# Group norm of a state-space stage: sums by a full block of ones, root and reciprocal on whole tiles

## The chip, the cores and the metric

One core of a Trainium2 chip runs the whole program. Its engines work side by side, each on its own instruction stream: TensorE (PE; PEld is its weight load), VectorE (DVE), ScalarE (ACT), GpSimd (POOL) and SyncE (SP, which issues the DMAs). They wait for each other by semaphores. The metric is the device time of one execution in microseconds (us).

## What is computed

The kernel is one step of a decoder layer for 512 new prompt tokens and 8 decode tokens (one for each of 8 sequences), so 520 tokens in all: an input norm and projection, sparse attention, a state-space branch (SSD) in 8 groups, a gated merge and a feed-forward part. The change lies in the norm at the end of the state-space branch. Each of its 8 groups has 256 channels, and each group is normalised by itself, token by token:

```python
y = y + d_skip.astype(F32).reshape(SSM_GROUPS, HEADS_PER_GROUP)[..., None] * xs
y = y.reshape(b, t, D_INNER) * jax.nn.silu(z.astype(F32))
yg = y.reshape(b, t, SSM_GROUPS, D_INNER // SSM_GROUPS)
yg = yg * lax.rsqrt(jnp.mean(yg * yg, axis=-1, keepdims=True) + EPS)
y = yg.reshape(b, t, D_INNER) * ssm_norm_w.astype(F32)
```

## The kernel before

Channels lie on the 128 partitions and the 520 tokens on the free axis, so a group's gated result `Y` is two tiles of 128x520, and a mean over channels is a sum over partitions, which TensorE makes by a matmul with ones.

The program is written by hand, one stream for each engine, and all streams have the same shape in this stage: a function `group(g, prev, more)`, called for group 0, then in a loop over groups 1 to 6, then for group 7. While group g's state work runs, TensorE also projects the six 128-channel tiles of group g + 1 (`D(0)` to `D(5)`, 8 steps of 128 rows each, two halves of 260 columns, f32, each half issued as two passes); in group 7 these are tiles for the merge gate. The order of the pieces is fixed by the order in the code.

A group runs like this. VectorE and ScalarE make the causal convolution (L1773, L1384) and the SiLU: a tanh on ScalarE (L1405) and a multiply on VectorE (L1780), four of each. GpSimd computes the convolution of the decode tokens (`dconv`, L2197 its last addition), for which the first tanh waits, and decays the decode states (L2202). TensorE turns B and the two x tiles by transposes (`step_turn`, L911 and L916), VectorE multiplies them by dt (`xdt`, L1791) and by the decay. TensorE spreads the decode tokens' B and C over the partitions (`step_decode`, L928); VectorE updates and reads the decode states (L1810 to L1824). TensorE multiplies C and B (`step_cb`, L936), VectorE masks the product (`CBm`, L1826). Then four chunks of 128 tokens: TensorE spreads the cumulative decay (`step_a`, L945), ScalarE makes exponentials of it (L1370 to L1374), GpSimd multiplies them with `CBm` (L2208), and TensorE forms the output and the state increment of the chunk (`step_y`, L958 to L964). VectorE carries the state `hT` from chunk to chunk: a copy for chunk 0 (L1835), a multiply and an add for the others (L1837, L1840); `step_y(c)` waits for the state of chunk c - 1. `Y` follows at the end (L1847 to L1855).

Between these pieces VectorE also runs four rounds of a top-8 search for the decode attention (`top`, L1734 to L1743), 12 pieces of 2.3 us, at fixed places: one piece behind the SiLU, two behind `xdt`, six behind `CBm`, three between the chunks.

The norm of group g - 1 runs inside group g. ScalarE squares the two `Y` tiles (L1379) and GpSimd adds them (L2175). TensorE sums over the partitions with the squares as weights and one column of ones as the moving operand (`sum_squares`, L410): the result is one number for each token, tokens on the partitions, five columns of PSUM. ScalarE takes the root of these 128x4 and 8x1 numbers (`root_norm`, L426), VectorE the reciprocal (`recip_norm`, L432). TensorE then spreads them back to all partitions (`spread_norm`, L418 and L419) and ScalarE copies the result out of PSUM into `rbg`, 128x520 (`copy_norm`, L436 and L437). VectorE multiplies `Y` by the gain and `rbg` (`norm`, L1756). On TensorE the sums stand behind `D(0)` and the spread behind `D(1)`, ahead of `step_turn`, since the x tiles are turned into the two PSUM banks that the norm uses.

Of the kernel before, what the change touches and what calls it, by code (L numbers as in the profile page):

```python
# [20 lines left out]
ACT = mybir.ActivationFunctionType  # L21
# [6 lines left out]
D = 1024  # L28
# [3 lines left out]
TH = T // 2  # L32
# [7 lines left out]
NG = 8  # L40
# [36 lines left out]
def build(nc, x_prompt, x_sample, cache_k, cache_v, cache_idx_k, state_ssm, state_conv, page_table,  # L77
# [5 lines left out]
    with ExitStack() as ctx:  # L83
# [22 lines left out]
        eps = sb("eps", [P, 1])  # L106
# [296 lines left out]
        NORM2, NORMF = NG + 1, NG + 2  # L403

# [29 lines left out]
        def copy_norm(act, e, out):  # L434
            act.wait_ge(S("norm_spread"), e + 1)
            act.activation(out[:, 0:SEQ], ps[:, 7, :], ACT.Copy).then_inc(S("norm_copied"), 1)  # L436
            act.activation(out[:, SEQ:T], ps[:, 6, 8:8 + NB], ACT.Copy).then_inc(S("norm_copied"), 1)  # L437
# [21 lines left out]
        def rms_dve(v, i, e, w_col):  # L459

            recip_norm(v, e)
            v.wait_ge(S("norm_copied"), 2 * e + 2)
# [208 lines left out]
        def _(pe):  # L671
# [229 lines left out]
            def step_norm(g):  # L901

                pe.wait_ge(S("sqg_added"), g + 1)
                sum_squares(pe, g + 1, sqg[:, 0, :])

            def step_turn(g, prev):
# [5 lines left out]
                if prev:  # L912
                    pe.wait_ge(S("norm_copied"), 2 * g + 2)
# [53 lines left out]
            def group(g, prev, more):  # L967
# [3 lines left out]
                D(0, 4, 8)  # L971
                if prev:
                    step_norm(g - 1)
                D(1)
                if prev:
                    spread_norm(pe, g)
# [32 lines left out]
            spread_norm(pe, NG)  # L1009
# [26 lines left out]
            pe.wait_ge(S("norm_copied"), 2 * NG + 2)  # L1036
# [194 lines left out]
        def _(act):  # L1231
# [148 lines left out]

            def group(g, prev, more):
# [16 lines left out]
                act.activation(dAs, ps[:, 4, 112:128].rearrange("p (i c) -> p i c", c=NB), ACT.Exp).then_inc(S("aux_read"), 1)  # L1398
                for i in range(4):
# [8 lines left out]
                if prev:  # L1408
                    root_norm(act, g, 256)
# [6 lines left out]
                if prev:  # L1416
                    copy_norm(act, g, rbg)
# [29 lines left out]
            root_norm(act, NG, 256)  # L1447
            copy_norm(act, NG, rbg)
# [124 lines left out]
        def _(v):  # L1573
# [178 lines left out]

            def norm(g):
                v.wait_ge(S("norm_copied"), 2 * g + 4)
# [5 lines left out]
            def group(g, prev, more):  # L1760
# [21 lines left out]
                if prev:  # L1782
                    recip_norm(v, g)
                    top(g, 0)
                    norm(g - 1)
                else:
                    top(g, 0)
# [29 lines left out]
                for j in range(2):  # L1817
                    v.wait_ge(S("state_new"), 2 * g + 2)
                    if j:
# [7 lines left out]
                                tri.unsqueeze(1).broadcast_to((P, 4, P)), ALU.mult).then_inc(S("CBm_ready"), 1)  # L1827
                top(g, 3, 4, 5, 6, 7, 8)
# [34 lines left out]
            recip_norm(v, NG)  # L1863
# [428 lines left out]
```

## Time and profile before

| what | us |
|---|---|
| time, median of 3 runs (1709.55 to 1717.97) | 1709.66 |
| the profiled execution | 1707.82 |
| its span, first to last instruction | 1706.0 |
| TensorE busy | 1612.1 (94%) |
| VectorE busy | 892.3 (52%) |
| ScalarE busy | 408.1 (24%) |
| GpSimd busy | 217.3 (13%) |

The span is cut at the first and the last instruction; the profiled execution's own time has 1.82 us around it. Busy time counts matmuls, weight loads and the like, not waiting. Matmul records overlap in the pipeline, so the distance of their starts, not their length, tells what one costs. TensorE's granted clock is the share of full speed that the chip gave it: 1.00 is 2.4 GHz, 0.50 is 1.2 GHz. A timeline row gives the start, the time to the end of the last of the merged instructions, the engine, the line, the operation, output<-input, form and count; in brackets stands the idle time of the engine before it and what ended it.

### The profile page before, as it was taken

Reading aid. Unit: us, or ns where it says so; the run is one execution under the profiler, and the core shown is the slowest. Engines: PE = TensorE matmul, PEld = TensorE weight load, DVE = VectorE, ACT = ScalarE, POOL = GpSimd, SP = SyncE. Lnnn points to the kernel's source line nnn. Section 1 sums busy time; section 2 is a strip of 40 time slices with the busy share of each in tenths; the row PEclk is TensorE's granted clock in tenths of the full one; section 3 lists DMA queues with packets and bytes.
Section 4 is the critical chain, followed back from the end, with each engine's and each line's share of the span. In section 5 each row is a group of like instructions: output and inputs, shape, how many; then the busy total and the mean of one; then the engine's idle time right before and its main releaser. Section 6 shows DMA issues by size and latency. Waiting matters only on the chain. (4 is left out here: it accounts for less than half of the span.)

```text
span 1706.0 us, 21649 instructions
## 1 busy us (share of the span) xinstructions
PE 1612.1 (94%) x8147; PEld 1366.3 (80%) x8147; DVE 892.3 (52%) x1412; ACT 408.1 (24%) x909; POOL 217.3 (13%) x224
## 2 busy tenths in 40 slices
PE   6998998899999899998998999999979999999997
PEld 5886786787877778777776888888868888888886
DVE  3313886349898898989987100010143444435232
ACT  3113316322243432434333011000112121210002
POOL 1000110022231322313222150000000000000000
PEclk7999999999999999999998999899989999999998
DMA  6111113123133131331212443212212232321211
GB/s 205 50 37 51 37 50 114 36 84 100 54 91 98 56 94 46 95 99 32 84 47 74 145 131 99 75 51 77 79 66 75 74 99 75 99 68 44 97 40 50
DMA packets 153489, 131.21 MB, mean 77 GB/s; under 512 B 11410, under 2 KB 149938, under 8 KB 153410
## 3 DMA queue, kind: packets, MB, share of 16 engines
q1 hardware_dynamic: 150610, 121.93, 23.6%
q0 software_dynamic: 2816, 8.39, 1.7%
q8 instruction: 46, 0.75, 0.2%
q14 instruction: 17, 0.14, 0.0%
HBM read 117.26 MB, written 13.27 MB: 77 GB/s over the span
## 5 line engine op out<-in xcount | busy, mean ns | idle before, releaser
L382 PE MATMUL ps<-xn,ring 128*128 128x260 f32 (+1 forms) x2752 | 635.7, 388 | 6.0 <-ACT work L1268 1.9
L382 PEld LDWEIGHTS ps<-xn,ring 128*128 128x128 f32 (+1 forms) x2752 | 521.3, 192 | 91.4 <-ACT work L1268 2.3
L1110 PE MATMUL ps<-xn,ring 128*128 128x260 f32 x528 | 124.8, 387 | 6.3 <-DVE xn L464 6.3
L1110 PEld LDWEIGHTS ps<-xn,ring 128*128 128x128 f32 x528 | 101.3, 192 | 22.1 <-issue 6.4
L382 PE MATMUL ps<-ssm_o,ring 128*128 128x260 f32 x512 | 114.6, 386 | 0.0
L382 PEld LDWEIGHTS ps<-ssm_o,ring 128*128 128x128 f32 x512 | 98.2, 192 | 15.2
L2208 POOL TENSOR_TENSOR ring<-ring 128x512 f32<-128x512 f32 x32 | 40.5, 1265 | 333.6 <-ACT ring L1374 333.6
L1110 PE MATMUL ps<-uT,ssm_o 128*128 128x260 f32 x352 | 81.1, 384 | 0.0
L1110 PEld LDWEIGHTS ps<-uT,ssm_o 128*128 128x128 f32 x352 | 67.3, 191 | 10.5
L1734 DVE MAX8 work<-work 8x8 f32<-8x2049 f32 x32 | 72.8, 2274 | 0.6
L1739 DVE FIND_INDEX8 dix<-work 8x8 uint32<-8x2049 f32 x32 | 72.8, 2274 | 0.0
L1741 DVE MATCH_REPLACE8 work<-work 8x2049 f32<-8x2049 f32 x32 | 72.5, 2266 | 0.0
L1523 ACT ACTIVATE uT<-ps 128x260 f32<-128x260 f32 x88 | 34.0, 387 | 154.3 <-PE ps L1110 154.3
L1773 DVE SCALAR_TENSOR_TENSOR work<-work 128x512 f32<-128x512 f32 x96 | 67.0, 768 | 7.3 <-ACT work L1384 7.3
L1872 DVE SCALAR_TENSOR_TENSOR work<-work 128x520 f32<-128x520 f32 x8 | 5.6, 700 | 118.7 <-ACT work L1464 118.7
L382 PE MATMUL ps<-uT,ring 128*128 128x260 f32 x256 | 58.8, 392 | 0.4 <-DVE uT L1922 0.4
L1161 PE MATMUL ps<-work,ring 128*128 128x260 f32 x264 | 59.2, 382 | 0.0
L2097 DVE TENSOR_TENSOR xT<-xT,ps 128x260 f32<-128x260 f32 x28 | 11.9, 424 | 86.2 <-PE ps L1161 86.2
L382 PEld LDWEIGHTS ps<-uT,ring 128*128 128x128 f32 x256 | 49.9, 196 | 8.5 <-DVE uT L1922 0.5
L1161 PEld LDWEIGHTS ps<-work,ring 128*128 128x128 f32 x264 | 50.2, 190 | 7.7
L382 PE MATMUL ps<-work,ring 128*128 128x260 f32 x256 | 56.3, 382 | 0.0
L1370 ACT ACTIVATE ring<-ps,work 128x128 f32<-128x128 f32 x128 | 36.5, 367 | 79.3 <-PE ps L945 79.3
(340 smaller groups left out, 2223.5 us busy)
## 6 DMA issues: line engine op xcount, KB each, us to landing
ring<-in_w_in SPq DMA_DIRECT2D x34, 1024.0 KB, 5.4
ring<-in_w_ffn_gate SPq DMA_DIRECT2D x11, 1024.0 KB, 5.3
ring<-in_w_ffn_up SPq DMA_DIRECT2D x11, 1024.0 KB, 5.3
ring<-in_w_in SPq DMA_DIRECT2D x16, 512.0 KB, 5.3
work<-in_state_ssm SPq DMA_DIRECT2D x16, 512.0 KB, 6.4
out<-work SPq DMA_DIRECT2D x16, 512.0 KB, 4.0
ring<-in_w_ssm_br SPq DMA_DIRECT2D x8, 1024.0 KB, 7.6
ring<-in_w_ffn_down SPq DMA_DIRECT2D x8, 1024.0 KB, 5.0
```

The lines of the kernel that those rows point to most:

```text
L382: mm = pe.matmul(ps[0:m, 2 * pair + h, 0:TH], lhs[k], rhs[k][:, h * TH:(h + 1) * TH], start=(k == 0), stop=(k == len(lhs) - 1))
L1110: mm = pe.matmul(ps[:, bank, 0:TH], lhs[:, k, :], rhs[:, k, :], start=start and k == 0, stop=k == 3, skip_group_check=not start)
L1161: mm = pe.matmul(ps[:, bank, 0:TH], lhs[k], rhs[k], start=start and k == 0, stop=k == KD - 1, skip_group_check=not start)
L1370: act.activation(M2[:, c % 2, r * P:(r + 1) * P], abc[:, r * P:(r + 1) * P], ACT.Relu, scale=-1.0, bias=atg[:, c, r:r + 1]).then_inc(S("E_ ...
L1523: act.activation(snap[:, i, :], ps[:, bank, 0:TH], ACT.Copy).then_inc(S("snapshot_taken"), 1)
L1734: v.max(best, row).then_inc(S("dtop_max"), 1)
L1739: v.max_index(dix[:], best, row).then_inc(S("dtop_index"), 1)
L1741: v.match_replace(row, best, row, -3.3e38).then_inc(S("dtop_cut"), 1)
L1773: v.scalar_tensor_tensor(xc[:, i, 0:SEQ], raw[:, i, t:t + SEQ], cw[:, 5 * i + t:5 * i + t + 1], xc[:, i, 0:SEQ], ALU.mult, ALU.add).then_i ...
L1872: v.scalar_tensor_tensor(m, gt, 1.0, m, ALU.add, ALU.mult).then_inc(S("mixed"), 1)
L2097: v.tensor_tensor(part, part, ps[:, bank, 0:TH], ALU.add).then_inc(S("down_added"), 1)
L2208: g.tensor_tensor(m, m, CBm[:, c:c + 1, :].broadcast_to((P, 4, P)), ALU.mult).then_inc(S("M_ready"), 1)
```

## The change

Per group, the sums are made by a full 128x128 block of ones as weights and the added squares as moving operand, 260 columns at a time, into PSUM banks 6 and 7 (`step_norm`). Every partition then holds the sum of every token, so no spread is needed. ScalarE takes the root from PSUM straight into `rbg` (`root_group`, two pieces of 128x260) and VectorE the reciprocal in place (`recip_group`, two pieces of 128x260), ahead of the same `norm`. `sum_squares`, `spread_norm` and the rest stay for the three other norms.

The pieces also move. On TensorE the sums now stand behind `step_aux`, ahead of the second half of `D(0)`, and the turn of the x tiles waits for the root alone. On ScalarE the root stands ahead of the four tanh, not behind them. On VectorE reciprocal and norm stand behind `CBm`, not ahead of `xdt`. Behind the last group the root, the reciprocal and the norm follow the sums as before, without the spread.

```diff
         NORM2, NORMF = NG + 1, NG + 2
+        SPREADS = {0: 1, NORM2: 2, NORMF: 3}
...
         def copy_norm(act, e, out):
-            act.wait_ge(S("norm_spread"), e + 1)
+            act.wait_ge(S("norm_spread"), SPREADS[e])
...
             def step_norm(g):
 
                 pe.wait_ge(S("sqg_added"), g + 1)
-                sum_squares(pe, g + 1, sqg[:, 0, :])
+                for h in range(2):
+                    mm = pe.matmul(ps[:, 6 + h, 0:TH], ones, sqg[:, 0, half[h]], start=True, stop=True)
+                mm.then_inc(S("norm_summed"), 1)
...
                 if prev:
-                    pe.wait_ge(S("norm_copied"), 2 * g + 2)
+                    pe.wait_ge(S("norm_root"), 2 * g + 2)
                 for c in range(4):
...
                 D(0, 0, 4)
                 step_aux(g, prev)
-                D(0, 4, 8)
                 if prev:
                     step_norm(g - 1)
+                D(0, 4, 8)
                 D(1)
-                if prev:
-                    spread_norm(pe, g)
                 step_turn(g, prev)
...
             step_norm(NG - 1)
-            spread_norm(pe, NG)
...
+            def root_group(g):
+
+                act.wait_ge(S("norm_summed"), g + 1)
+                for h in range(2):
+                    act.activation(rbg[:, half[h]], ps[:, 6 + h, 0:TH], ACT.Sqrt, scale=1.0 / 256,
+                                   bias=eps[:, 0:1]).then_inc(S("norm_root"), 1)
+
...
                 act.activation(dAs, ps[:, 4, 112:128].rearrange("p (i c) -> p i c", c=NB), ACT.Exp).then_inc(S("aux_read"), 1)
+                if prev:
+                    root_group(g)
                 for i in range(4):
...
                 act.activation(wexp, wexp, ACT.Exp).then_inc(S("wexp_ready"), 1)
-                if prev:
-                    root_norm(act, g, 256)
...
-                if prev:
-                    copy_norm(act, g, rbg)
                 act.wait_ge(S("turned"), g + 1)
...
+            def recip_group(g):
+
+                v.wait_ge(S("norm_root"), 2 * g + 2)
+                for h in range(2):
+                    v.reciprocal(rbg[:, half[h]], rbg[:, half[h]]).then_inc(S("norm_recip"), 1)
+
             def norm(g):
-                v.wait_ge(S("norm_copied"), 2 * g + 4)
+                v.wait_ge(S("norm_recip"), 2 * g + 4)
...
-                if prev:
-                    recip_norm(v, g)
-                    top(g, 0)
-                    norm(g - 1)
-                else:
-                    top(g, 0)
+                top(g, 0)
...
                                 tri.unsqueeze(1).broadcast_to((P, 4, P)), ALU.mult).then_inc(S("CBm_ready"), 1)
+                if prev:
+                    recip_group(g)
+                    norm(g - 1)
                 top(g, 3, 4, 5, 6, 7, 8)
...
-            recip_norm(v, NG)
+            recip_group(NG)
             norm(NG - 1)
```

TensorE in the loop over groups 1 to 6, from the last transposes of `step_aux` to the turn, before (L382 are the tiles; `ps` is PSUM, `work` and `cst` hold the squares, the ones and the identity):

```order
L898 MATMUL ps<-cst,work 128x128 x2
L382 MATMUL ps<-xn,ring 128x260 x8
L410 MATMUL ps<-cst,work 128x1 [waits sqg_added]
L410 MATMUL ps<-cst,work 128x1 x3
L410 MATMUL ps<-cst,work 8x1
L377 REGISTER_ALU
L382 MATMUL ps<-xn,ring 128x260 [waits dense_read]
L382 MATMUL ps<-xn,ring 128x260 x15
L416 ISA
L418 MATMUL ps<-cst,rt 128x128 [waits norm_recip]
L418 MATMUL ps<-cst,rt 128x128 x3
L419 MATMUL ps<-cst,rt 128x8
```

The same place after the change:

```order
L899 MATMUL ps<-cst,work 128x128 x2
L906 MATMUL ps<-work,cst 128x260 [waits sqg_added]
L906 MATMUL ps<-work,cst 128x260
L382 MATMUL ps<-xn,ring 128x260 x8
L377 REGISTER_ALU
L382 MATMUL ps<-xn,ring 128x260 [waits dense_read]
L382 MATMUL ps<-xn,ring 128x260 x15
L912 REGISTER_ALU [waits ctok_ready]
L914 MATMUL ps<-cst,work 128x128 [waits silu_done]
L914 MATMUL ps<-cst,work 128x128 x3
L916 ISA
L919 MATMUL ps<-cst,work 128x128 [waits norm_root]
```

The sums have moved up by 8 matmuls and are two instead of five; the five spread matmuls with their wait for the reciprocal are gone, and the turn waits for the root.

VectorE in the same loop, from the SiLU multiplies to the `xdt` products, before:

```order
L1780 SCALAR_TENSOR_TENSOR work<-work 128x520 [waits th_ready] x4
L432 RECIPROCAL rt<-rt 128x4 [waits norm_root]
L432 RECIPROCAL rt<-rt 8x1
L1734 MAX work<-work 8x8 [waits dtop_cut]
L1754 ISA
L1756 ISA [waits norm_copied]
L1756 REGISTER_ALU
L1756 SCALAR_TENSOR_TENSOR ssm_o<-work,cwg 128x520
L1756 ISA
L1756 REGISTER_ALU
L1756 SCALAR_TENSOR_TENSOR ssm_o<-work,cwg 128x520
```

After the change the same stretch reads, with `xdt` (L1796) right behind the search:

```order
L1790 SCALAR_TENSOR_TENSOR work<-work 128x520 [waits th_ready] x4
L1738 MAX work<-work 8x8 [waits dtop_cut]
L1794 REGISTER_ALU
L1796 TENSOR_TENSOR xdt<-ps,work 128x512 [waits turned]
L1796 TENSOR_TENSOR xdt<-ps,work 128x512
```

Reciprocal and norm, with their waits for the root and the copy, have left this place.

VectorE further on in the group, from `CBm` (L1826, L1831 after the change) to the search behind it, before:

```order
L1826 TENSOR_TENSOR ring<-ps,cst 128x512 [waits cb_done]
L1734 MAX work<-work 8x8 [waits dtop_cut]
L1739 MAX_INDEX dix<-work 8x8 [waits dtop_max,dtop_kept]
L1741 MATCH_REPLACE work<-work 8x2049
L1743 ISA [waits dtop_index]
```

and after:

```order
L1831 TENSOR_TENSOR ring<-ps,cst 128x512 [waits cb_done]
L1761 RECIPROCAL work<-work 128x260 [waits norm_root]
L1761 RECIPROCAL work<-work 128x260
L1764 ISA
L1766 ISA [waits norm_recip]
L1766 REGISTER_ALU
L1766 SCALAR_TENSOR_TENSOR ssm_o<-work,cwg 128x520
L1766 ISA
L1766 REGISTER_ALU
L1766 SCALAR_TENSOR_TENSOR ssm_o<-work,cwg 128x520
L1738 MAX work<-work 8x8 [waits dtop_cut]
```

The two reciprocals, now 128x260, and the norm stand between the mask and the searches.

## Rows read from the trace of the kernel before

**Rows 1.** Windows by group: stretch, length, busy by engine, PEclk, DMA share, GB/s.

```profile
430.61:857.73 427.12, 401.78 (x2318) 337.49 (x2317) 387.72 (x457) 150.42 (x343) 116.53 (x108) 0.98 0.28 78
430.61:500.75 70.14, 67.18 (x388) 56.08 (x387) 64.56 (x77) 25.09 (x58) 19.41 (x18) 0.98 0.29 80
```

**Rows 2.** Waits, 390 to 936 us: who waited for whom, total, times, longest.

```profile
PE ps L418 <- DVE rt L432: 20.0, 7, 3.1
```

**Rows 3.** Timeline of TensorE in one group, 575 to 642 us.

```profile
575.17 3.67 PE L382 MATMUL ps<-xn,ring 128*128 128x260 f32 x16
...
590.06 1.35 PE L418 MATMUL ps<-cst,rt 128*128 128x128 f32 x8 [3.10 <-DVE rt L432]
...
594.40 7.18 PE L382 MATMUL ps<-xn,ring 128*128 128x260 f32 x32
601.42 3.73 PE L928 MATMUL ps<-cst,work 128*128 128x128 f32 x32
...
629.04 0.45 PE L958 MATMUL ps<-ring,xdt 128*64 128x128 f32 x4
...
636.60 0.70 PE L964 MATMUL ps<-ring 128*128 128x256 f32 x2
```

**Rows 4.** Timeline of VectorE in the same group.

```profile
587.97 0.70 DVE L1780 SCALAR_TENSOR_TENSOR work<-work 128x520 f32<-128x520 f32 x1 [0.15 <-ACT work L1405]
...
589.93 2.27 DVE L1734 MAX8 work<-work 8x8 f32<-8x2049 f32 x1
592.92 1.43 DVE L1756 SCALAR_TENSOR_TENSOR ssm_o<-work,cwg 128x520 f32 x2 [0.71 <-ACT work L437]
594.60 1.29 DVE L1791 TENSOR_TENSOR xdt<-ps,work 128x512 f32<-128x512 f32 x2 [0.26 <-PE ps L916]
...
603.40 1.22 DVE L1810 TENSOR_TENSOR ring<-ps,work 128x1024 f32<-128x1024 f32 x1 [1.51 <-PE ps L928]
...
613.56 0.69 DVE L1826 TENSOR_TENSOR ring<-ps,cst 128x512 f32<-128x512 f32 x1
...
616.63 0.08 DVE L1739 MATCH_VALUE_LOAD dix<-work 8x8 f32 x1 [0.18 <-DVE work L1734]
...
628.45 0.40 DVE L1835 COPY work<-ps 128x256 f32<-128x256 f32 x1
...
637.47 0.41 DVE L1837 TENSOR_TENSOR work<-work 128x256 f32<-128x256 f32 x1
```

**Rows 5.** Line L1620, a reciprocal on a whole tile: ns min/median/max, first and last start.

```profile
L1620 DVE RECIPROCAL work<-work x1: 3403/3403/3403, 105.6 to 105.6; 128x520 f32<-128x520 f32 x1
```

**Rows 6.** Line L1780, and the timeline of GpSimd at two places.

```profile
L1780 DVE SCALAR_TENSOR_TENSOR work<-work x32: 685/699/2389, 375.4 to 873.6; 128x520 f32<-128x520 f32 x32
...
573.38 1.29 POOL L2175 TENSOR_TENSOR work<-work 128x520 f32<-128x520 f32 x1 [7.17 <-ACT work L1379]
...
618.29 1.26 POOL L2208 TENSOR_TENSOR ring<-ring 128x512 f32<-128x512 f32 x1 [31.64 <-ACT ring L1374]
```

**Rows 7.** Windows around stretches at half clock, columns as in rows 1.

```profile
587.48:590.89 3.41, 0.83 (x7) 0.83 (x8) 2.14 (x5) 3.22 (x7) 0.00 (x0) 1.00 0.75 230
590.89:594.31 3.42, 3.42 (x17) 3.06 (x17) 2.71 (x3) 0.67 (x2) 0.00 (x0) 0.50 0.23 77
...
921.99:932.23 10.24, 8.69 (x42) 6.63 (x43) 6.68 (x12) 0.94 (x2) 2.49 (x2) 0.50 0.01 2
```

**Rows 8.** Timeline of ScalarE in the same group, 575 to 590 us.

```profile
582.04 1.17 ACT L1405 ACTIVATE work<-work 128x520 f32<-128x520 f32 x2 [4.75 <-POOL work L2197]
...
588.07 1.28 ACT L426 ACT_TABLE_LOAD   x1
...
589.67 0.58 ACT L1344 ACTIVATE work<-ps 128x520 f32<-128x520 f32 x1
```

**Rows 9.** Timeline of TensorE behind the last group.

```profile
935.66 1.18 PE L410 MATMUL ps<-cst,work 128*128 128x1 f32 x10 [1.94 <-POOL work L2175]
...
939.42 29.73 PE L382 MATMUL ps<-ssm_o,ring 128*128 128x260 f32 x128
```

More of the change, by code:

```diff
@@ L461, in rms_dve @@
             recip_norm(v, e)
-            v.wait_ge(S("norm_copied"), 2 * e + 2)
+            v.wait_ge(S("norm_copied"), 2 * SPREADS[e])
             for k in range(KT):
@@ L1034, in _ @@
             sbr(2, 0)
-            pe.wait_ge(S("norm_copied"), 2 * NG + 2)
+            pe.wait_ge(S("norm_root"), 2 * NG + 2)
             pe.wait_ge(S("decode_read"), POS_READ)
@@ L1446, in _ @@
             group(NG - 1, True, False)
-            root_norm(act, NG, 256)
-            copy_norm(act, NG, rbg)
+            root_group(NG)
             act.wait_ge(S("aux_done"), NG + 1)
```

## The prediction

> **What bounds the kernel now.** The page's busy shares mix unlike stages, so I went from them to the table of windows, cut at the same instruction of each state group: six groups take 427.12 us, and in the first of them TensorE works 67.18 and VectorE 64.56 of 70.14 us [rows 1]. Both are nearly full here, and work taken off one is worth only what the other allows.
>
> The list of waits names the stall of TensorE: 20.0 us in seven waits of the spread matmuls for VectorE's reciprocal [rows 2]. The timeline of one group shows it: TensorE stands 3.10 us before L418, the spread starts at 590.06 and the next tile at 594.40 [rows 3]. In the same group VectorE loses 1.26 us between its last SiLU multiply (ends 588.67) and the search at 589.93, then 0.71 and 0.26 us around the norm, and 1.51 us for the first half of the L928 matmuls; from there to the copy of the state at 628.45 its longest gap is 0.18 us [rows 4]. That copy is what step_y(1) on TensorE waits for: it ends at 628.85, and L958 starts at 629.04 [rows 3, 4]. The two engines meet there with next to no slack, so a later copy is a later group.
>
> **Part 1, TensorE.** The five one-column sums take 1.18 us [rows 9]. Two 260-column matmuls of two passes each take 4 x 0.219 = 0.88 us, since a tile of 32 passes lasts 7.02 us, 594.40 to 601.42 [rows 3]. The sums now stand half a tile earlier, at 575.17, behind the aux step; GpSimd's add of the squares ends at 573.38 + 1.29 = 574.67 [rows 3, 6], so this wait still finds its work done, by 0.5 us. The spread matmuls go, and so does the wait for the reciprocal: the turn now needs the root and the third SiLU multiply, which ends 0.15 us before the row at 587.97, at 587.82 [rows 4]. Twelve transposes at full clock take 12 x 3.73/32 = 1.4 us by the row of L928, so they end at 589.2 and the next tile at 596.3 instead of 601.42: 5.1 us earlier.
>
> **Part 2, ScalarE.** The root moves ahead of the four tanh. It costs a table load to Sqrt and one back, 1.28 us each, and two reads of 260 columns, each under the 0.58 us of a 520-column read: below 3.8 us. ScalarE idles there 4.75 us, waiting for GpSimd's decode convolution [rows 8]. The load that the Exp of the chunks needed is no longer wanted, so there are still two a group. I cost this at nothing; the cover is that idle time, and beyond it every tanh would start late by the excess. The copies of the norm out of PSUM go, off the path.
>
> **Part 3, VectorE.** Two small reciprocals go. Two on 128x260 come: 3403 ns for 128x520 [rows 5] makes 2 x 1.70 = 3.40 us. The norm's pair (1.43 us) moves from before the xdt products to behind CBm. Queued behind these 4.83 us are two rounds of the top-8 search and then the state copy that TensorE waits for. Walk the group, in the clock of the rows. The search starts at 588.67 instead of 589.93 and ends at 590.94; xdt starts there instead of at 594.60, 3.66 earlier. From xdt to the product that reads L928 lie 8.80 us, 1.51 of them waiting, so VectorE is ready at 598.2; TensorE's first half of L928, 1.98 us behind the tile's end at 596.3, comes at 598.3. So that product starts 5.1 earlier, and CBm ends at 609.15 instead of 614.25 [rows 4]. Then come 4.83 us that were not there: 613.98. The searches take their old 14.20 us, and the copy starts at 628.2, against 628.45. **What TensorE gains, 5.1 us, VectorE gives back, 4.83 us.**
>
> One term can add to this. GpSimd's first multiply of the chunk ran 1.26 us from 618.29, 4.04 us behind CBm's end [rows 6], with a table load of 1.28 on the way to it that now leaves; so it would run from 2.8 to 4.0 us behind CBm. The norm, whose two tiles both lie in SBUF, starts at 3.4: they would overlap by 0.6 us. A SiLU multiply, two SBUF tiles as well, has a median of 699 ns and a maximum of 2389 [rows 6], so such a wait is possible; the cost lies between 0 and 0.6. The Trainium skill (SBUF — State Buffer, "Who interferes with whom") says that a VectorE instruction with two SBUF inputs and a GpSimd instruction that reads SBUF exclude each other, and that the later one blocks fully; by it the whole overlap would be paid. The copy moves by -0.25 to +0.35 us. I take 0, near the middle: the group stays at the 71.40 us of part 4 before any new effect of the clock.
>
> **Part 4, where the stall goes.** TensorE now reaches step_y(1) at 629.04 - 5.1 = 623.9 and gets the copy at about 628.7: one wait of 4.8 us in place of the 3.1. The granted clock matters here. The wait before L418 is followed by a stretch of 3.4 us at 0.50, the level of 1.2 GHz, in five of the seven groups, and of 6.8 us in a sixth ([rows 7] show one: TensorE worked 0.83 of the 3.41 us before it fell). The first group escaped and took 70.14 us, against (427.12 - 70.14)/5 = 71.40 for the next five [rows 1]: a stretch cost 1.26 us there. In the last group, whose step_y's leave TensorE waiting, it was at half for 10.24 us, busy 8.69 of them [rows 7]. Behind the new wait stand 8.26 us of TensorE work, from 629.04 to the end of L964 at 637.30; VectorE takes its result at 637.47 [rows 3, 4], and step_y(1) started 0.19 behind the copy, so about 0.3 us of lateness is free. One stretch of 3.4 us at half loses 1.7, that is 1.4 net; two in a row lose 3.4, 3.1 net. The middle is 2.25; with one in seven that escapes, 2.25 x 6/7 = **1.9 us for each group.**
>
> The Trainium skill (TensorE: Matmul & The Clock Gate, "What's actually happening") says that the slow clock is the default and that activity lifts it. Read strictly, none would escape: 2.25 a group, 2.1 us more over six. Against it stands the one group of this trace that did.
>
> **Part 5, the end.** In the last group the step_y's already wait and run at half clock; I take no change. Behind it, from the sums to the branch product, lie 935.66 to 939.42 = 3.76 us [rows 9]; sums of 0.88 and two transposes that fit in 0.7 remain: 2.2 us less. The late reciprocal and norm, 4.83 us, hide behind the first 14 of 16 steps of that product, 14 x 0.88 = 12 us. From there on TensorE's work runs on as before.
>
> **Sum.** Six groups: 6 x (71.4 + 1.9) = 439.8 against 427.12, +12.7; the end -2.2: **+10.5 us**. The profiled execution took 1707.82 us (span 1706.0, 1.82 around it): 1718.3. The median of the runs shown, 1709.66, lies 1.84 above that execution: **1720.2**.
>
> **Rivals.**
> 1. The exchange alone: the clock does not fall with the new wait, or its stretch is over before the copy comes. For it: one group escaped. Against it: the new wait is half as long again. 6 x 71.4 = 428.4, +1.3, less 2.2: -0.9, 1708.8. This ends on the other side, not slower.
> 2. VectorE is not the bound: if the reciprocals found free time on it, the 5.1 us would stay gained: 7 x 5.1 + 2.2 = 38 us, 1671.8, or half of it if half fits. It decides at 4.83 us of idle VectorE between CBm and the copy; the rows show gaps of 0.18 there [rows 4]. This is what the change promises.
> 3. Contention on top of the clock: the norm is held by GpSimd's multiply and two stretches at half follow: 71.4 + 0.35 + 3.1 = 74.85; 6 x 74.85 = 449.1, +22.0 - 2.2 = +19.8, 1729.5.
>
> **How the numbers follow.** Forecast 0.65; in it a price of 1.4 to 3.1 spans 1717.2 to 1727.4. Rival 1 0.21, rival 2 0.05, rival 3 0.09. Half a per cent, 8.5 us, is about what a measurement of this kernel can tell from no change. Slower by more: most of the forecast (0.52) and rival 3, 0.61. Within: the lower edge of the forecast (0.13) and rival 1, 0.34. Faster by more: rival 2, 0.05. The range takes the forecast, rival 1 with the copy 0.25 us early (6 x 71.15 = 426.9, -0.2 - 2.2 = -2.4, 1707.3) and the edge of rival 3: 1707 to 1728.
>
> **What would show it.** Right: little of a wait left before the turn (under 1 us: TensorE is done with its tile at 587 and SiLU at 587.8); TensorE's list of waits headed by step_y for the state copy, near 4.8 us in each of seven groups; VectorE busy near 68 us a group; a granted clock of 0.50 behind that wait and none in the turn; groups of 73 us. Wrong: reciprocals well off 1.70 us; tanh starting late behind the table loads; no stretch at half clock in the groups (rival 1); VectorE idle between CBm and the copy (rival 2).

## The result

The changed kernel takes **1730.47 us** (median of 6 runs, 1729.52 to 1731.31). The kernel before, run beside it, takes 1712.58 us (6 runs, 1704.45 to 1719.5). The ratio is 1.0103, with a 95% interval of 1.0072 to 1.0135: slower by 17.9 us. The forecast was slower by 10.5 us, 1720.2 in a range of 1707 to 1728. The sign came as forecast; the size lies outside the range.

The profiled execution took 1729.71 us, with a span of 1727.9 against 1706.0 before, and a granted TensorE clock of 0.954 against 0.965 over the span.

### The profile page after: what moved, and what is told of

Read it like the earlier page. It is cut to its first block and busy times, and to the rows that moved or that the text cites. A ratio compares the mean times of both kernels' runs of the same rounds, so it can differ in the third digit from the quotient of the medians.

```text
span 1727.9 us, 21377 instructions
## 1 busy us (share of the span) xinstructions
PE 1613.3 (93%) x8019; PEld 1364.1 (79%) x8019; DVE 912.8 (53%) x1412; ACT 405.7 (23%) x893; POOL 217.4 (13%) x224
## 5 line engine op out<-in xcount | busy, mean ns | idle before, releaser
L382 PE MATMUL ps<-xn,ring 128*128 128x260 f32 (+1 forms) x2752 | 639.0, 390 | 6.0 <-ACT work L1268 1.9
L382 PEld LDWEIGHTS ps<-xn,ring 128*128 128x128 f32 (+1 forms) x2752 | 525.8, 193 | 94.1 <-issue 2.5
L382 PE MATMUL ps<-ssm_o,ring 128*128 128x260 f32 x512 | 116.1, 390 | 0.0
L382 PEld LDWEIGHTS ps<-ssm_o,ring 128*128 128x128 f32 x512 | 99.2, 194 | 15.7
L1110 PEld LDWEIGHTS ps<-uT,ssm_o 128*128 128x128 f32 x352 | 67.2, 191 | 10.5
L961 PE MATMUL ps<-ring,xdt 128*64 128x128 f32 x256 | 31.2, 329 | 44.7 <-DVE work L1843 35.0
L961 PEld LDWEIGHTS ps<-ring,xdt 128*64 128x64 f32 x256 | 18.7, 157 | 56.6 <-issue 43.1
L382 PE MATMUL ps<-uT,ring 128*128 128x260 f32 x256 | 58.4, 390 | 0.4 <-DVE uT L1930 0.4
L382 PE MATMUL ps<-work,ring 128*128 128x260 f32 x256 | 56.3, 382 | 0.0
```

The costliest lines, as they stand in the source:

```text
L382: mm = pe.matmul(ps[0:m, 2 * pair + h, 0:TH], lhs[k], rhs[k][:, h * TH:(h + 1) * TH], start=(k == 0), stop=(k == len(lhs) - 1))
L961: pe.matmul(o, xdt[:, c, 64 * r:64 * r + 64], M2[:, c % 2, r * P:(r + 1) * P], start=True, stop=(c == 0))
L1110: mm = pe.matmul(ps[:, bank, 0:TH], lhs[:, k, :], rhs[:, k, :], start=start and k == 0, stop=k == 3, skip_group_check=not start)
```

## The profile after

First the table of windows, cut where the six groups start and end, as in [rows 1], then three of the groups. The columns are the stretch, its length, the busy time of TensorE, its weight loads, VectorE, ScalarE and GpSimd, the granted clock, the DMA share and GB/s.

```profile
431.74:877.39 445.65, 402.17 (x2222) 334.93 (x2221) 402.03 (x457) 148.64 (x330) 116.52 (x108) 0.94 0.26 74
...
505.18:580.80 75.62, 68.22 (x372) 56.65 (x371) 66.98 (x77) 24.75 (x56) 19.41 (x18) 0.93 0.26 73
...
654.58:727.33 72.75, 65.30 (x372) 54.63 (x371) 67.02 (x77) 24.75 (x56) 19.42 (x18) 0.98 0.27 76
727.33:804.44 77.11, 69.70 (x372) 57.54 (x371) 66.97 (x77) 24.75 (x55) 19.41 (x18) 0.91 0.26 72
```

Six groups take 445.65 us instead of 427.12: 74.3 each, from 72.75 to 77.11 (the rows left out: 73.44, 73.78 and 72.95). VectorE is busy 67.0 us in every one of them; what varies is the granted clock, and the group with the lowest clock (0.91) is the longest (77.11). The work is the same each time, so the 4.4 us between the shortest and the longest group come from the clock.

Next the waits from 390 to 936 us: who waited for whom, total, times, longest. The last row is from the kernel before.

```profile
PE ps L961 <- DVE work L1843: 35.0, 7, 5.0
DVE work L1845 <- PE ps L967: 27.0, 13, 6.6
ACT L1414 <- POOL work L2205: 18.1, 7, 2.6
```

```profile
DVE work L1837 <- PE ps L964: 8.4, 9, 3.3
```

TensorE's 20.0 us before the spread matmuls [rows 2] are gone. In their place it waits 5.0 us in each of seven groups for the copy of the state (L1843) before step_y(1) (L961). And VectorE waits 27.0 us, where it waited 8.4 before (L1837), for its next state: that (L1845) needs the last product of step_y(2) or step_y(3) (L967).

The timelines of one group show how one wait makes the other. First TensorE, then VectorE, in the changed kernel.

```profile
562.07 0.70 PE L961 MATMUL ps<-ring,xdt 128*64 128x128 f32 x4 [5.00 <-DVE work L1843]
...
568.88 4.25 PE L382 MATMUL ps<-xn,ring 128*128 128x260 f32 x12
```

```profile
542.14 3.40 DVE L1761 RECIPROCAL work<-work 128x260 f32<-128x260 f32 x2
545.83 1.50 DVE L1766 SCALAR_TENSOR_TENSOR ssm_o<-work,cwg 128x520 f32 x2 [0.28 <-DVE work L1761]
...
561.51 0.41 DVE L1843 COPY work<-ps 128x256 f32<-128x256 f32 x1
...
574.87 0.42 DVE L1845 TENSOR_TENSOR work<-work 128x256 f32<-128x256 f32 x1 [5.11 <-PE ps L967]
```

Read them together. VectorE delivers the copy at 561.9. TensorE, idle for 5.00 us, starts step_y(1) at 562.07; the twelve tile matmuls at 568.88 take 4.25 us. VectorE has finished its search and stands 5.11 us until step_y(2) is through. The granted clock says why: the windows of three such stretches, in three groups.

```profile
561.41:571.65 10.24, 9.58 (x37) 7.45 (x38) 8.14 (x11) 2.14 (x6) 0.44 (x1) 0.50 0.00 0
711.59:715.01 3.42, 3.42 (x20) 2.81 (x20) 3.25 (x3) 0.00 (x0) 0.00 (x0) 0.50 0.00 0
783.27:796.93 13.66, 12.71 (x46) 9.52 (x48) 8.44 (x11) 2.43 (x7) 2.49 (x2) 0.50 0.00 0
```

At 0.50 TensorE is at 1.2 GHz, half its full clock. The stretch of 3.42 us lies in the group of 72.75 us, that of 10.24 in the group of 75.62, that of 13.66 in the group of 77.11. Against the 71.4 us that the prediction used for a group without this effect, they cost 1.35, 4.2 and 5.7 us.

The profiled spans differ by 21.9 us. Cut at the squares of the first group, at those of the seventh, and at the branch product (939.42 before [rows 9], 956.48 after), the parts of it are: ahead of the stage +1.1, six groups +18.5, the last group with its tail -2.6, all behind +4.8.

## The experiments

Two theories stood at the start. **A, clock:** what VectorE gives back cancels what TensorE gains, and the loss is the half-clock stretch behind the new wait. **B, work:** the reciprocals' 3.4 us on VectorE are the loss, and the clock only accompanies it. Code is shown in part; `...` marks what is left out.

### no_recip: the reciprocals left out

```
             def recip_group(g):
 
-                v.wait_ge(S("norm_root"), 2 * g + 2)
-                for h in range(2):
-                    v.reciprocal(rbg[:, half[h]], rbg[:, half[h]]).then_inc(S("norm_recip"), 1)
+                pass
 
             def norm(g):
-                v.wait_ge(S("norm_recip"), 2 * g + 4)
+                v.wait_ge(S("norm_root"), 2 * g + 4)
```

> The changed kernel without the two reciprocals of a group (the norm multiplies by the root itself, so the reciprocal is left out of the result). Theory A, clock: the copy of the state comes 3.4 us earlier, step_y(1) waits about 1.5 us instead of 5.0, TensorE no longer falls to half clock behind it, and a group drops from 74.3 us by 3.4 us of VectorE and by the 2.9 us of clock, to 68: about 1686 us in all. Theory B, work: only VectorE's own 3.4 us leave a group, the clock stretches are a bystander: 7 x 3.4 = 24 us less, about 1706 us.

Measured: 1689.47 us (4 runs), 0.9865 of the kernel before (0.9835 to 0.9895). The windows of the six groups, of a stretch in the first and of the second:

```profile
432.40:843.85 411.45, 385.19 (x2222) 322.95 (x2221) 389.81 (x445) 148.65 (x330) 116.52 (x108) 0.99 0.29 81
487.03:490.44 3.41, 3.41 (x19) 2.71 (x16) 3.23 (x3) 0.00 (x0) 0.37 (x1) 0.50 0.00 0
502.53:570.79 68.26, 63.68 (x372) 53.42 (x371) 65.08 (x75) 24.75 (x55) 19.42 (x18) 1.00 0.29 81
```

The waits of TensorE for the copy of the state in it:

```profile
PE ps L961 <- DVE work L1841: 14.4, 7, 2.1
```

The wait is 2.1 us instead of 5.0. In groups 2 to 6 the clock stays at 1.00, and a group takes 68.26 us: 6 us less for 3.4 us less of VectorE. The first group falls to 0.50 for 3.41 us behind the same wait. The time is nearer A's number, but work and clock went together here; the next run parts them.

### fill_after: the wait filled with spare matmuls

```
+            def fill(g, n):
+
+                pe.wait_ge(S("dense_read"), 6 * g + N_SSM + 11)
+                for i in range(n):
+                    pe.matmul(ps[:, i % 2, 0:TH], ident, xn[:, 0, 0:TH], start=True, stop=True)
...
                 D(5, 2, 4)
+                if prev:
+                    fill(g, 10)
                 step_y(g, 1)
```

> The changed kernel with ten spare 260-column matmuls (4.4 us) on TensorE ahead of step_y(1), into two PSUM banks that are free there; they compute nothing that is used. VectorE's work is untouched. Theory A, clock: TensorE works through the wait, stays at 1.00 behind it, groups go from 74.3 to about 71.4 us, 6 x 2.9 = 17 us less: about 1713 us. Theory B, work: the lateness comes from VectorE, the spare matmuls change nothing or cost: 1730 us or more.

Measured: 1712.41 us (12 runs, 1706.14 to 1713.9), 0.9999 of the kernel before (0.9984 to 1.0015). The windows of the second group and of a stretch at the start of the third; then, in the second group, TensorE and the instruction of VectorE that had been late.

```profile
503.38:574.91 71.53, 69.54 (x392) 58.43 (x391) 67.67 (x77) 24.89 (x55) 19.43 (x18) 0.98 0.28 78
578.62:582.03 3.41, 3.41 (x10) 2.64 (x9) 3.41 (x7) 3.38 (x11) 2.15 (x4) 0.50 0.14 39
```

```profile
555.44 4.55 PE L974 MATMUL ps<-xn,cst 128*128 128x260 f32 x20
560.60 0.45 PE L961 MATMUL ps<-ring,xdt 128*64 128x128 f32 x4 [0.61 <-DVE work L1851]
...
564.24 2.90 PE L382 MATMUL ps<-xn,ring 128*128 128x260 f32 x12
...
569.01 0.41 DVE L1853 TENSOR_TENSOR work<-work 128x256 f32<-128x256 f32 x1
```

TensorE now does 4.55 us of useless work in each group and the kernel is 18 us faster than the changed one (1730.47 - 1712.41). The same twelve matmuls take 2.90 us instead of 4.25, and VectorE no longer waits for step_y(2). VectorE's work is untouched, so B falls as an account of the loss: **nearly all that the groups lost against the kernel before is what the clock took behind this wait** (six groups of 429.2 us, against 445.7 in the changed kernel and 427.1 before). Without that, the change is worth nothing either way, as the exchange in the prediction had it (71.53 us a group here; 71.4 there). Not every stretch at half clock is gone: one of 3.41 us now stands at the start of each group, from the sums on. It costs little there, for a group without any takes 71.22 us (in fill_half below). Against no_recip, 71.53 - 68.26 = 3.27 us a group is what 3.40 us of reciprocals cost without the stretch behind step_y(1): VectorE sets most of the group.

### fill_before: the same in the old wait

```
                 if prev:
+                    pe.wait_ge(S("ctok_ready"), g + 1)
+                    for i in range(7):
+                        pe.matmul(ps[:, 5, 0:TH], ident, xn[:, 0, 0:TH], start=True, stop=True)
                     spread_norm(pe, g)
```

> The kernel before with seven spare 260-column matmuls (3.1 us) on TensorE in the wait for the reciprocal, ahead of the spread, into a bank that the turn overwrites. Theory A, clock: no stretch at half clock behind that wait; the groups take the 70.14 us of the one that escaped, 6 or 7 x 1.26 = 8 us less than the kernel before: about 1704 us. Theory B: the spread starts no earlier, so no change, or up to 0.5 us a group more where the spare matmuls end late.

Measured: 1711.69 us (12 runs), 0.9999 of the kernel before (0.9981 to 1.0017): no gain, where A expected some 8 us less. TensorE in one group, up to the spread, and VectorE around it:

```profile
510.38 5.36 PE L382 MATMUL ps<-xn,ring 128*128 128x260 f32 x16
...
523.70 3.23 PE L978 MATMUL ps<-xn,cst 128*128 128x260 f32 x14
526.76 1.05 PE L418 MATMUL ps<-cst,rt 128*128 128x128 f32 x8
...
524.99 0.21 DVE L432 RECIPROCAL rt<-rt 128x4 f32<-128x4 f32 x2 [1.12 <-ACT rt L426]
529.12 1.43 DVE L1759 SCALAR_TENSOR_TENSOR ssm_o<-work,cwg 128x520 f32 x2 [1.72 <-ACT work L437]
```

Its groups take 71.53 us (the profiled execution was the longest of the twelve, 1719.38 us). The half-clock stretch behind the spread is gone, but another stands earlier in the group (the half tile at 510.38 takes 5.36 us, against 3.67 in [rows 3]), so the filling starts late; the reciprocal is there at 525.2, and the spread waits for the spare matmuls until 526.76. VectorE then stands 1.72 us before the norm. The test overran its own wait, and what a stretch costs in the kernel before stays undecided by it.

### fill_half: half the filling

The changed kernel with `fill` as in fill_after, but half as many:

```
                 D(5, 2, 4)
+                if prev:
+                    fill(g, 5)
                 step_y(g, 1)
```

> The changed kernel with 5 spare matmuls of 260 columns ahead of step_y(1), where 10 were tried. They cover about 2 of the 5.0 us, so that some 3 us of waiting stay. Theory A, if a wait of 3 us leaves the clock alone: groups of 71.5 us, 1712 us. Theory A, if 3 us are enough for a half-clock stretch of the shortest kind seen (3.41 us): groups of about 72.7 us, 1720 us. Theory B: 1729 to 1731 us.

Measured: 1721.77 us (4 runs), 1.006 (1.0039 to 1.0081). Three groups in a row:

```profile
504.28:576.92 72.64, 67.38 (x382) 56.54 (x381) 68.10 (x77) 24.75 (x55) 19.43 (x18) 0.98 0.27 76
576.92:648.14 71.22, 65.88 (x382) 55.33 (x381) 67.68 (x77) 24.76 (x56) 19.43 (x18) 1.00 0.28 78
648.14:723.75 75.61, 70.39 (x382) 58.59 (x381) 66.98 (x77) 24.75 (x55) 19.43 (x18) 0.93 0.26 73
```

The same wait of 2.8 us is left in each of these groups, and what follows is a short stretch, none, or a long one. The group of 71.22 us shows the bare work without any stretch, and the price in the others is 1.4 and 4.4 us. The time answers to the second number of A (1720 us), but as a mean of unlike groups (73.2 us) and not by one short stretch in each.

### in_three: the same work in three portions

```
                 if prev:
-                    recip_group(g)
-                    norm(g - 1)
+                    recip_group(g, 0)
                 top(g, 3, 4, 5, 6, 7, 8)
...
                     if c == 0:
+                        if prev:
+                            recip_group(g, 1)
                         top(g, 9, 10)
                     if c == 1:
+                        if prev:
+                            norm(g - 1)
                         top(g, 11)
```

> The same instructions as the changed kernel on every engine; only VectorE's order differs: the first reciprocal stays behind the mask of C and B, the second goes behind the copy of the state, the norm behind the second state. Theory A (clock): TensorE's one wait of 5.0 us at step_y(1) becomes about 1.9 us there and 1 to 3 us at step_y(2) and step_y(3); these are about the waits that the kernel without reciprocals keeps at full clock, so the half-clock stretches go, a group takes 71.5 us, and the time is about 1712 us. Theory B (VectorE's work, or the sum of TensorE's waits, sets the time): 1729 to 1731 us, as the changed kernel.

Measured: 1718.94 us (6 runs), 1.0043 (1.0028 to 1.0058), between the two expectations. TensorE at step_y(1) and step_y(3) of one group, and the window of that group:

```profile
558.51 0.70 PE L961 MATMUL ps<-ring,xdt 128*64 128x128 f32 x4 [2.07 <-DVE work L1842]
...
571.16 0.45 PE L961 MATMUL ps<-ring,xdt 128*64 128x128 f32 x4 [2.83 <-DVE work L1847]
...
504.03:576.61 72.58, 67.35 (x374) 56.19 (x373) 66.54 (x77) 24.91 (x56) 19.19 (x18) 0.95 0.27 76
```

Order alone gave back 11.5 of the 18 us: the stretches are shorter (3.4 us each), one to three in a group and twelve in the six. A's assumption that a wait of 2.07 us leaves the clock alone, taken from no_recip, does not hold: four matmuls of L961 take 0.70 us here right behind such a wait, and 0.45 at full clock. Nor did it hold in no_recip's own first group. The length of a wait alone does not say what the clock does.

### one_recip: one of the two reciprocals left out

```
-                for h in range(2):
-                    v.reciprocal(rbg[:, half[h]], rbg[:, half[h]]).then_inc(S("norm_recip"), 1)
+                v.reciprocal(rbg[:, half[0]], rbg[:, half[0]]).then_inc(S("norm_recip"), 1)
+                v.sem_inc(S("norm_recip"), 1)
```

> The second reciprocal of every group is left out of the result, so VectorE has 1.7 us less work a group; the other stays. Between the changed kernel (groups of 74.3 us) and the one without reciprocals (68.27 us). Theory A: the work takes 1.6 us off, 71.5 to 69.9 us, and TensorE's wait falls to about 3.4 us; at full clock that makes about 1701 us, with one short half-clock stretch a group about 1709 us. Theory B (no clock in it, 6 us per 3.4 us of VectorE work in proportion): 71.3 us a group, about 1710 us; the trace tells the two apart by whether step_y runs at half clock.

Measured: 1721.66 us (4 runs), 1.0066 (1.0044 to 1.0087), far above every expectation (1701 to 1710). VectorE, then GpSimd, behind CBm:

```profile
542.66 2.47 DVE L1766 SCALAR_TENSOR_TENSOR ssm_o<-work,cwg 128x520 f32 x2 [0.28 <-DVE work L1760]
...
543.31 1.26 POOL L2216 TENSOR_TENSOR ring<-ring 128x512 f32<-128x512 f32 x1 [25.07 <-ACT ring L1374]
```

1.7 us of reciprocal went, but in all six groups the norm that now starts earlier meets GpSimd's first multiply of the chunk and takes 2.47 us instead of 1.50: 0.7 us is saved, not 1.7. TensorE still waits 29.3 us in seven groups for the copy, 4.2 each, and the groups take 72.1 us, two of them 75.0. This is the meeting that the prediction had priced for the changed kernel at 0 to 0.6 us; there it cost less than 0.1 (a norm of 1.50 us against 1.43 [rows 4]). The Trainium skill's rule (SBUF — State Buffer, "Who interferes with whom") that such a pair exclude each other, the later one blocked in full, agrees with the row: the norm grows by about 1 us, most of the multiply's 1.26. In the changed kernel the rows overlap by 0.27 us (the multiply ends at 546.10, the norm starts at 545.83) and the norm grows by 0.07, less than that rule would give.

### old_place and norm_late: the place

old_place puts the changed kernel's reciprocals and norm ahead of the xdt products; norm_late moves only the norm, in the kernel before.

```
                 top(g, 0)
+                if prev:
+                    recip_group(g)
+                    norm(g - 1)
                 v.wait_ge(S("turned"), g + 1)
...
-                if prev:
-                    recip_group(g)
-                    norm(g - 1)
                 top(g, 3, 4, 5, 6, 7, 8)
```

> The changed kernel with its reciprocals and norm ahead of the product of x and dt, where the norm stood before, in place of behind the mask of C and B. The same work on every engine. Theory A (VectorE's sum and the clock): nothing lies idle ahead of that product any more that could cover 4.8 us, so the copy of the state is as late as in the changed kernel, TensorE's wait at step_y(1) is about 5 us, a group takes 73.5 to 75 us, and the time is 1727 to 1733 us. Theory C (the place costs: up to 3.4 us of it would be covered there): groups of 71.3 us or less and 1705 to 1712 us.

```
                     recip_norm(v, g)
                     top(g, 0)
-                    norm(g - 1)
...
+                if prev:
+                    norm(g - 1)
                 top(g, 3, 4, 5, 6, 7, 8)
```

> The kernel before with one edit: the norm's two products (1.43 us) go behind the mask of C and B, as in the changed kernel; sums, spread matmuls, small roots and reciprocals stay. Theory A: ahead of the product of x and dt VectorE then waits for the transposes instead, the copy of the state is 1.4 us later, and TensorE, which still waits 2.9 us a group for the small reciprocals, waits some 1.4 us more at step_y(1): groups of about 72.7 us at full clock and about 1718 us, up to 1727 us with a half-clock stretch a group behind step_y(1). Theory C (TensorE's time, not VectorE's, sets the group): groups of 71.4 us and 1710 us.

Measured: old_place 1729.43 us, 1.0121 (1.0095 to 1.0148); norm_late 1730.87 us, 1.0129 (1.0102 to 1.0155), 4 runs each. The main wait of TensorE in old_place and the window behind it in the second group; then, in norm_late, from VectorE's timeline of one group, xdt, the casts behind the search and the second state; last, such a cast in the kernel before.

```profile
PE ps L939 <- DVE ring L1829: 29.1, 8, 4.1
...
544.58:554.82 10.24, 8.51 (x27) 7.10 (x28) 9.00 (x9) 2.15 (x6) 1.26 (x1) 0.50 1.09 277
```

```profile
528.88 1.29 DVE L1790 TENSOR_TENSOR xdt<-ps,work 128x512 f32<-128x512 f32 x2 [2.38 <-PE ps L916]
...
556.76 0.46 DVE L1743 CAST work<-dix 8x8 uint32 x1
...
564.13 0.84 DVE L1743 CAST work<-dix 8x8 uint32 x1
...
575.34 0.47 DVE L1838 TENSOR_TENSOR work<-work 128x256 f32<-128x256 f32 x1 [2.20 <-PE ps L964]
```

```profile
628.38 0.15 DVE L1743 CAST work<-dix 8x8 uint32 x1
```

In old_place the time is A's, but the wait is not where A put it: TensorE stands 4.1 us before the products of C and B (L939) and 0.8 before the decode spread (L931), and finds the copy ready later. The lack of 5 us in a group is the same, only at other instructions. A half-clock stretch follows there too, 10.24 us in groups 2 to 6 and 6.83 in the first, and the six groups take 449.88 us, 75.0 each.

norm_late is the surprise: 1.42 us of work, moved and not added, cost some 22 us (1.0129), as much as the whole change. Its six groups take 448.67 us, 74.8 each. VectorE stands 2.38 us before xdt, as expected, where the norm was. From the start of xdt to the copy at 564.90 it takes 36.02 us, where it took 33.85 [rows 4]: the norm's 1.3 to 1.4, and most of a microsecond in two casts, which now fall beside GpSimd's multiplies and take 0.46 and 0.84 us in place of 0.15. Behind the copy a half-clock stretch of 3.41 us follows, and VectorE stands 2.20 us for step_y(2). The expected 72.7 us at full clock left both out; the expected upper end, 1727 us, had the stretch but not the casts. In both runs theory C, as each expectation has it, falls: the groups take 75.0 and 74.8 us, not 71.4.

### after_again, before_again, before_third: how steady the stretches are

The kernels unchanged, each for another profile.

> The changed kernel once more, for a second profile: is the length of the half-clock stretches behind step_y(1) a matter of the execution or of the kernel? Theory A, with the price of 2.9 us a group a property of the kernel: the six groups sum to 440 to 450 us again (445.6 in the first profile), with stretches of 3.4 to 13.7 us mixed again, and the time is 1729 to 1732 us. If the first profile was an unlucky one, the groups come near the forecast's 73.3 us each, 440 us in all, and the time near 1724 us.

> The kernel before, unchanged, for a second profile: its runs so far spread from 1704 to 1719 us. If a half-clock stretch in the stage of the keys (absent from the first profile, present in that of the changed kernel) makes that spread, a profiled time above 1712 us shows one there and one below 1710 us shows none; if it is the groups that vary, a group differs from 71.3 to 71.5 us.

> The kernel before, unchanged, for a third profile. In the first (1707.82 us) the stage of the keys stayed at full clock, in the second (1716.75 us) it was at half for 13.7 us, with the same 427 to 428 us for the six groups. A time near 1709 us with that stretch in it would say that the stage does not make the spread of its runs; a time near 1709 us without it, or above 1714 us with it, that it does.

Measured: 1728.33, 1716.75 and 1710.98 us. The six groups of after_again; then a block of the keys stage (L1059) in the kernel before (first profile), in before_again and in the changed kernel.

```profile
430.36:876.01 445.65, 402.18 (x2222) 334.98 (x2221) 402.03 (x457) 148.64 (x331) 116.51 (x108) 0.94 0.26 75
```

```profile
1011.60:1022.80 11.20, 10.95 (x100) 10.70 (x100) 0.70 (x1) 5.27 (x9) 5.67 (x6) 1.00 0.28 83
...
1013.80:1029.10 15.30, 15.05 (x99) 14.80 (x99) 0.70 (x1) 5.27 (x9) 5.67 (x6) 0.71 0.22 62
...
1027.20:1043.40 16.20, 15.95 (x98) 15.70 (x99) 0.70 (x1) 5.27 (x9) 5.68 (x6) 0.66 0.20 58
```

The six groups repeat to a hundredth: 445.65 us both times, and the time, 1728.33, lies just under the expected 1729. So the price of 2.9 us a group was no bad draw; it belongs to this kernel. In the keys stage the same block takes 11.2 us at full clock and 15.3 to 16.2 with a half-clock stretch. Two of three profiles of the kernel before escape it (1707.82 and 1710.98 us; in before_third the block takes 11.1 us) and one does not (1716.75); both of the changed kernel have it. So have the other variants, no_recip and ln_exp too, but not old_place and norm_late, which are as slow as the changed kernel and stay at full clock there. It goes with no part of the change that could be named, and what brings it on is open.

### ln_exp: the reciprocal taken off VectorE

```
                 for h in range(2):
-                    act.activation(rbg[:, half[h]], ps[:, 6 + h, 0:TH], ACT.Sqrt, scale=1.0 / 256,
+                    act.activation(rbg[:, half[h]], ps[:, 6 + h, 0:TH], ACT.Ln, scale=1.0 / 256,
                                    bias=eps[:, 0:1]).then_inc(S("norm_root"), 1)
+                act.wait_ge(S("norm_root"), 2 * g + 2)
+                for h in range(2):
+                    act.activation(rbg[:, half[h]], rbg[:, half[h]], ACT.Exp, scale=-0.5).then_inc(S("norm_recip"), 1)
...
             def recip_group(g):
 
-                v.wait_ge(S("norm_root"), 2 * g + 2)
-                for h in range(2):
-                    v.reciprocal(rbg[:, half[h]], rbg[:, half[h]]).then_inc(S("norm_recip"), 1)
+                pass
```

> The changed kernel with the reciprocal root made on ScalarE as an exponential of minus half the logarithm: Ln in place of Sqrt, two Exp of 128x260 behind it, no reciprocal on VectorE. Theory A, clock: as without the reciprocals, groups of 68 us, about 1686 us, if the two table loads and four reads (4.1 us) stay within ScalarE's idle 4.75 us ahead of the first tanh. Theory B, work: about 1706 us. A third reading, ScalarE late: each tanh starts late and the time stays above 1706 us.

Measured: **1690.5 us** (4 runs, 1690.44 to 1691.08), 0.9873 of the kernel before (0.9843 to 0.9903). It beats both kernels, by 19 us and by 40. ScalarE in one group, and the window of the six:

```profile
512.15 0.73 ACT L1389 ACTIVATE work<-work 128x260 f32<-128x260 f32 x2
513.42 1.16 ACT L1417 ACTIVATE work<-work 128x520 f32<-128x520 f32 x2 [0.54 <-POOL work L2206]
...
433.30:844.76 411.46, 385.19 (x2222) 322.92 (x2221) 389.83 (x445) 153.03 (x343) 116.53 (x108) 0.99 0.29 81
```

The second pass of 0.73 us, with a table load of 1.28 us ahead of it, fits into ScalarE's idle time, with 0.54 us of it left before tanh. The groups take 411.46 us, where no_recip, with no reciprocal at all, takes 411.45: the reciprocal has become free.

## Why the prediction was right and wrong

Five rows that the list uses. In the changed kernel, from the group behind the one above: the next tile on TensorE, then on VectorE the last SiLU multiply and the copy of the state. In the first group of the kernel before: the window of a stretch, and the spread.

```profile
598.00 6.30 PE L382 MATMUL ps<-xn,ring 128*128 128x260 f32 x28
...
596.73 0.70 DVE L1790 SCALAR_TENSOR_TENSOR work<-work 128x520 f32<-128x520 f32 x1 [0.15 <-ACT work L1414]
...
637.15 0.41 DVE L1843 COPY work<-ps 128x256 f32<-128x256 f32 x1
```

```profile
433.88:437.29 3.41, 3.41 (x10) 2.65 (x9) 3.41 (x6) 1.98 (x9) 1.69 (x4) 0.50 0.10 27
...
448.62 1.16 PE L418 MATMUL ps<-cst,rt 128*128 128x128 f32 x8 [1.41 <-DVE rt L432]
```

- **Part 1, TensorE: right.** From the last SiLU multiply to the next tile lay 5.7 us before [rows 3, 4]; now the tile starts at 598.00, 0.6 us behind it: the forecast 5.1 us are gained. The wait left before the turn is 7.0 us in six groups, 1.2 each, a little over the "under 1 us" of the forecast.
- **Part 2, ScalarE: right.** It still waits 2.6 us for GpSimd before tanh in each of seven groups, so the root is covered.
- **Part 3, VectorE: right.** Reciprocals 3.40 us, norm 1.50 for 1.43. From the end of the SiLU multiplies to the copy it was 39.78 us and is 39.72 (597.43 to 637.15): the exchange is even, and fill_after shows it as a time, 0.9999 of the kernel before. Rival 2 fell with it.
- **Part 4, the place and length of the wait: right; its price: wrong.** 5.0 us before step_y(1) in each of seven groups, against 4.8.
- **The step that failed, the price of that wait.** It was put at 1.9 us a group: one stretch of 3.4 us or two, and one group in seven without. A single stretch cost 1.35, as forecast (1.4). But the stretches of the six groups lasted 6.83, 10.24, 6.83, 3.42, 13.66 and 6.82 us, and none escaped: 74.28 - 71.4 = 2.9 us a group, 6 x 1.0 more than in the sum. Two factors were mis-sized. The first is the length, some 0.6 of the 1.0. The one row that showed a longer stretch, 10.24 us in the last group [rows 7], was named as what follows the waits of step_y, but the price was taken from the spread's short stretches, at another place in the group. The second is the escape, some 0.3. The first group before did not pass the same wait at full clock: it had been at half clock earlier in the group, came later to the spread and waited 1.41 us there, where the others waited 3.1. The forecast's discount of one in seven, rival 1's support and the price "a stretch cost 1.26 us there" all rest on this group. The Trainium skill (TensorE: Matmul & The Clock Gate, "What's actually happening") says that the slow clock is the default and that activity lifts it. Read strictly, as the prediction put it, no group would escape; none of these six did, but groups 2 to 6 of no_recip, behind 2.06 us, did. Why one stretch is longer than another stays open.
- **Part 5, the end of the stage: right.** -2.6 us, against -2.2.
- **"From there on TensorE's work runs on as before": wrong, by 4.8 us.** The block of the keys stage shown above took 16.2 us instead of 11.2.
- **The sum on the profiled executions:** forecast +10.5; +5.8 for the longer stretches, +4.8 for the keys, +1.1 ahead of the stage, which had been left out, and -0.4 at the end make +21.8, against 21.9 measured between the spans. The medians lie only 17.9 apart, since the profiled execution of before, without the stretch in the keys stage, was among its shorter ones.

Rival 3 named 1729.5 us, close to the result, with groups of 74.85, but half of its reason was not there: GpSimd held the norm for less than 0.1 us. Its other half, two stretches behind one wait, was. That it came so near is luck: the keys stage (+4.8) was not in it.

## What to carry to other kernels

Where two engines hand work to and fro with no slack, time saved on one is worth only what the other can follow. Here VectorE's 4.83 us took back the 5.1 us a group that TensorE gained, and 3.4 us less of VectorE was worth, with the clock, 6. Price a new TensorE wait by the stretches at half clock that follow waits at that very place, from the row of the worst one too, and look at who waits for the engine while it is slow. Before taking a part that did better as the sample, check that it met the same wait. A full-tile reciprocal on a loaded VectorE is a candidate for the Ln and Exp of an engine with idle time.

## What the runs showed of the chip

- Half-clock stretches behind one and the same kind of wait lasted 3.4 to 13.7 us, in a pattern that repeated between two executions of the kernel (445.65 us both times). TensorE was busy 9.58 of 10.24 us in one and still at 0.50.
- A wait of about 2.07 us before the same step was followed by full clock in groups 2 to 6 of no_recip, and by half clock in its first, in four of the six groups of in_three and in all six of norm_late. What decides is left open.
- A half-clock stretch is not dear everywhere: in fill_after one of 3.41 us stands at the start of each group, and the groups take 71.53 us, against 71.22 for one without any in fill_half.
- Useless matmuls in a wait made the kernel 18 us faster than without them; half as many made it only 9 faster, with groups of 71.2 to 75.6 us.
- Beside GpSimd's multiplies a cast of 0.15 us on VectorE took 0.84, and the norm's pair 2.47 instead of 1.50, so moving an instruction can cost more than its length.
